# Tokens stationary in every projection, features reached by a trip through device memory, and VectorE for the gate product of the second MLP

## What is computed

```
h = h + stick_breaking_mixer(rms_norm(h, norm_mix), sb_w_qkv, sb_w_o)      # 16 heads of 128
h = h + square(relu(rms_norm(h, norm_mlp) @ mlp_w1)) @ mlp_w2             # 2048 -> 8192 -> 2048
x = rms_norm(h, final_norm)
z = rms_norm(x, pre_mix_g_2) @ w_in_2                                     # q, k, v: 1024 each, pool: 1024
m = concat(chunked_attention(q, k, v, rel_bias_2), multiscale_pool(u)) @ w_o_2
x = x + rms_norm(m, post_mix_g_2)
up = causal_dwconv(rms_norm(x, pre_ffn_g_2) @ w_up_2, conv_w_2, conv_b_2)  # 2048 -> 2 x 5632
y = (gelu(up[:5632]) * up[5632:]) @ w_down_2
out = x + rms_norm(y, post_ffn_g_2)
```

## Time and profile before

| | |
|---|---|
| median of 3 runs | 2119.08 us (2118.93 to 2119.95) |
| profiled execution, first to last instruction | 2117.7 us |
| TensorE busy | 2110.5 us (100%), 10990 matmuls |
| VectorE, ScalarE, GpSimd busy | 1259.2, 1049.5, 189.2 us |
| moved by DMA | 415.11 MB, mean 196 GB/s |

### The profile page before, as it was taken

One profiled execution on the slowest core, in us unless ns is written; L12 is line 12 of the kernel. 1 busy time (PEld: TensorE's weight loads), 2 busy tenths in 40 slices (PEclk: granted clock), 3 DMA queues, 4 the chain that ended last, 5 costly groups with the idle time before them and its releaser, 6 DMA issues.

```text
span 2117.7 us, 26776 instructions
## 1 busy us (share of the span) xinstructions
PE 2110.5 (100%) x10990; PEld 1810.4 (85%) x10990; DVE 1259.2 (59%) x1341; ACT 1049.5 (50%) x1222; POOL 189.2 (9%) x90
## 2 busy tenths in 40 slices
PE   9999999999999999999999999999999999999998
PEld 8888888888888888888888888888888888888887
DVE  6555656656455555465667755576666644566565
ACT  7554555544334443344555635465455443455543
POOL 3000000000000000000004000002222100222210
PEclk9999999999999999999999999999999999999999
DMA  8565557765666666666676567655655666556663
GB/s 289 171 207 172 180 169 232 223 195 174 209 193 183 199 211 191 186 193 195 219 238 189 178 210 228 195 183 173 195 191 178 217 191 192 182 175 199 204 210 120
DMA packets 220363, 415.11 MB, mean 196 GB/s; under 512 B 13521, under 2 KB 23889, under 8 KB 219729
## 3 DMA queue, kind: packets, MB, share of 16 engines
q1 hardware_dynamic: 219376, 408.92, 61.3%
q10 hardware_dynamic: 864, 4.49, 0.6%
HBM read 405.49 MB, written 7.86 MB: 195 GB/s over the span
## 4 chain that ended last, share of the span: by engine, by line
PE 100%; ACT 0%; DVE 0%; issue 0%; POOL 0%; DVEq 0%; POOLq 0%
PE ps L1503 99%; PE ps L1506 0%; ACT T L1075 0%; DVE QK L1390 0%; ACT raw L1088 0%; ACT aHL L954 0%; ACT zs L1085 0%; DVE rs L1407 0%; POOL ones L1434 0%; ACT rs L1080 0%; POOL ident L1432 0%; DVE rs L1404 0%; DVE rs L1409 0%; DVE rs L1399 0%; POOL tri L1433 0%
## 5 line engine op out<-in xcount | busy, mean ns | idle before, releaser
L1146 DVE TENSOR_TENSOR Wl<-raw,Wh 128x1024 fp32r<-128x1024 f32 x743 | 911.8, 1246 | 640.6 <-ACT Wh L930 639.9
L1503 PE MATMUL ps<-aHL,Wh 128*128 128x512 f32 x3336 | 1158.7, 392 | 0.5 <-ACT aHL L954 0.4
L930 ACT ACTIVATE Wh<-raw 128x1024 fp32r<-128x1024 f32 x743 | 767.6, 1054 | 588.9 <-PE ps L1503 585.4
L1503 PE MATMUL ps<-aHL,Wl 128*128 128x256 f32 x3328 | 929.3, 279 | 0.0
L1503 PEld LDWEIGHTS ps<-aHL,Wh 128*128 128x128 f32 x3336 | 624.2, 187 | 139.5 <-issue 0.9
L1503 PEld LDWEIGHTS ps<-aHL,Wl 128*128 128x128 f32 x3328 | 628.2, 189 | 0.5
L1503 PE MATMUL ps<-Wh,hid 128*128 128x512 f32 x1728 | 533.1, 389 | 0.0
L1503 PEld LDWEIGHTS ps<-Wh,hid 128*128 128x128 f32 x1728 | 324.4, 188 | 67.5
L1503 PE MATMUL ps<-Wl,hid 128*128 128x512 f32 x864 | 336.2, 389 | 0.0
L1503 PEld LDWEIGHTS ps<-Wl,hid 128*128 128x128 f32 x864 | 162.2, 188 | 33.5
L1503 PE MATMUL ps<-Wh,oHL 128*128 128x512 f32 x512 | 158.7, 389 | 0.0
(11 more groups left out here) (175 smaller groups left out, 792.2 us busy)
## 6 DMA issues: line engine op xcount, KB each, us to landing
raw<-in_mlp_w_dram SPq DMA_DIRECT2D x256, 512.0 KB, 4.3
raw<-in_w_up_dram SPq DMA_DIRECT2D x176, 512.0 KB, 3.9
raw<-in_sb_w_qkv_dram SPq DMA_DIRECT2D x93, 512.0 KB, 4.8
raw<-in_w_down_dram SPq DMA_DIRECT2D x88, 512.0 KB, 4.2
raw<-in_w_in_dram SPq DMA_DIRECT2D x64, 512.0 KB, 4.4
raw<-in_sb_w_o_dram SPq DMA_DIRECT2D x32, 512.0 KB, 5.3
raw<-in_w_o_dram SPq DMA_DIRECT2D x32, 512.0 KB, 4.3
passed_rows<-xN SPq DMA_DIRECT2D x16, 256.0 KB, 4.3
```

The costliest lines, as they stand in the source:

```text
L930: e.activation(Wh[:, i % NW, :], rawv[:, i % NRAW, :], ACT.Copy).then_inc(st["hi"][0], 1)
L1146: e.tensor_tensor(Wl[:, i % NW, :], rawv[:, i % NRAW, :], Wh[:, i % NW, :].bitcast(F32), ALU.subtract).then_inc(st["lo"][0], 1)
L1503: return e.matmul(o, l, r, start=start, stop=stop, skip_group_check=True)
```

## The change

All strips are of kind N. The column groups of the weights that feed q, k, the pool and both up projections are permuted on the host, and their results leave PSUM by a trip: ScalarE copies the token rows, scaled by a column of norm factors (or relu, then square), to T0; SP writes them to device memory (`passed_strip`, two slots); two pieces later SP reads them back in blocks into T0; two pieces after that VectorE transposes T0 into QK, T1 or E. One trip may be on its way at a time; a second one is put off until the first has landed. Rows r_a and r_b, `diagonal`, `spread` and the "wide" products go. Columns scaled by QSCALE are made beside the norm factors.

PSUM is cut anew: two sets of two banks for strips, one of four banks for side work and the pool's own piece. Scores, weights and values move back by three pieces (five for the first group). The output projections and w_down run the first two strips as a pair: both strips' pieces but the last two, then those two of each. `mixed_norm` and the turns after w_o_2 use the side set. In the second MLP VectorE makes the gate product, the steps of the convolution move closer together, and the halves follow one piece later, as before.

The diff, cut to its core:

```diff
     def side_set():
-        return 1 - now[0]
+        return 2
+    def strip_pair(w, s4, ks, tail, mov, tiles, evacs, koff=0):
+        first, n = len(p.pieces), len(ks) - tail
+        for i in range(2):
+            strip(w, (s4 + i) * STRIP, ks, mov, tiles, evacs[i], koff)
+        a, b = p.pieces[first:first + len(ks)], p.pieces[first + len(ks):]
+        p.pieces[first:] = a[:n] + b[:n] + a[n:] + b[n:]
+        return first
...
+    def trip(s, k, n, how, col, need, landed_to):
+        if st.get("landing"):
+            st["landing"].append(lambda: trip(s, k, n, how, col, need, landed_to))
+            return
+        st["landing"] = [lambda: landed_to(moved)]
...
+        step("stage_rows", n=n, set=s, mm=k, how=how, col=col, need=need, t0_free=list(free["T0"]), staged=staged, squared=squared,
+             passed=passed, held=st.get(("trip", n % 2)))
+        st["trip", n % 2] = moved
+        free[f"set{s}"] = [staged[1]]
+        free["T0"] = [moved]
+        def back():
+            step("land_rows", n=n, passed=passed, done=moved)
+            later(2, landed)
...
+        later(2, back)
...
-    after(13, r_job("r1", "a", "r_a"))
+    after(13, lambda: rms("r1", "a"))
...
-        after(first["v", g] + 1, sb_scores(g))
-        after(first["v", g] + 8, sb_weights(g))
-        after(first["v", g] + 12, values(g, 1))
+        at = first["v", g] + (0 if g else 2)
+        after(at + 4, sb_scores(g))
+        after(at + 11, sb_weights(g))
+        after(at + 15, values(g, 1))
...
-        after(first2["v", g] + 1, sm_scores(g))
-        after(first2["v", g] + 10, sm_turn(g))
-        after(first2["v", g] + 12, values(g, 2))
+        after(first2["v", g] + 4, sm_scores(g))
+        after(first2["v", g] + 13, sm_turn(g))
+        after(first2["v", g] + 15, values(g, 2))
...
-        ps = [ctx.enter_context(nc.psum_tensor(f"ps{i}", [128, 4, 512], F32)) for i in range(2)]
+        ps = [ctx.enter_context(nc.psum_tensor(f"ps{i}", [128, n, 512], F32)) for i, n in enumerate((2, 2, 4))]
...
+                elif k == "stage_rows":
+                    if st["held"]:
+                        e.wait_ge(*st["held"])
+                    for t in range(2):
+                        e.wait_ge(*(st["squared"] or st["staged"])[t])
+                        e.dma_start(passed_strip[st["n"] % 2, t * 128:(t + 1) * 128, :], strip_rows[:, t, :]).then_inc(st["passed"][0], 16)
+                elif k == "land_rows":
+                    e.wait_ge(*st["passed"])
+                    for a in range(4):
+                        e.dma_start(strip_landed[a * 32:(a + 1) * 32, :, :],
+                                    passed_strip[st["n"] % 2].rearrange("(c j) (a f) -> a j c f", c=8, a=4)[a]).then_inc(st["done"][0], 16)
...
+                elif k == "turn_strip":
+                    for t in st["need"]:
+                        e.wait_ge(*t)
...
+                    e.transpose(dst, strip_blocks).then_inc(st["done"][0], 1)
...
-                elif k == "gate":
-                    e.tensor_tensor(E4, E4, Z4, ALU.mult).then_inc(st["done"][0], 1)
+                elif k == "gate":
+                    e.tensor_tensor(E4, E4, Z4, ALU.mult).then_inc(st["done"][0], 1)
...
-                    for m in range(4):
-                        c = slice(t * 512 + m * 128, t * 512 + (m + 1) * 128)
-                        mm(P[:, m, :], wh[:, c], x, q["first"] and t == 0, False)
-                        r = mm(P[:, m, 0:TOK], wl[:, c], x[:, 0:TOK], False, q["last"] and t == 1)
+                    for row in range(2):
+                        hi = mov[:, kt + t, row * 128:(row + 1) * 128]
+                        lo = mov[:, kt + t, TOK + row * 128:TOK + (row + 1) * 128]
+                        mm(P[:, row, :], hi, wh[:, c], q["first"] and t == 0, False)
+                        mm(P[:, row, :], hi, wl[:, c], False, False)
+                        m = mm(P[:, row, :], lo, wh[:, c], False, False)
```

More of the change, by code:

```diff
@@ L140, in row_pair @@
         second = dict(root=done("rms_root"), rec=done("rms_rec"), sq=done("rms_rec"), prod=done("rms_rec"), r=done("rms_r"))
[L141 to L145, removed]
+        both, scaled = done("rms_r"), done("rms_r")
+        step("row_pair", need=st["rows_sq"], total=total, mean=mean, first=first,
+             square=square, moved=moved, mean2=mean2, second=second, both=both, scaled=scaled)
+        st["r3c"], st["r4c"] = first["r"], scaled
     def turn(n, gain_name, need):
@@ L169, in turn_blocks @@
             tile_hl[4 * n:4 * n + 4] = lo
+            waiting, st["moving"] = st["moving"][1:], []
+            for job in waiting:
+                job()
         later(3 if n == 3 else 4, turn_blocks)
[L172 to L183, removed]
+    def trip(s, k, n, how, col, need, landed_to):
+        if st.get("landing"):
+            st["landing"].append(lambda: trip(s, k, n, how, col, need, landed_to))
+            return
+        st["landing"] = [lambda: landed_to(moved)]
+        staged = [done("rows_staged") for t in range(2)]
+        squared = [done("rows_squared_up") for t in range(2)] if how == "relu" else None
+        passed, moved = done("strip_passed", 32), done("strip_moved", 4 * 16)
+        step("stage_rows", n=n, set=s, mm=k, how=how, col=col, need=need, t0_free=list(free["T0"]), staged=staged, squared=squared,
[6 more added lines that the diff above has]
+            later(2, landed)
+        def landed():
+            first, *others = st["landing"]
+            st["landing"] = []
+            first()
+            for job in others:
+                job()
+        later(2, back)
@@ L191, in common, with evac_qk, landed, go @@
         return summed, kw
-    def evac_qk(which, g, scale, r, rname):
+    def evac_qk(which, g, col, rname):
+        n = next_trip()
         def f(s, k):
[L195 to L203, removed]
+            def landed(moved):
+                turned = done("qk_turned")
+                step("turn_strip", to="qk", g=g, which=which, need=[moved, *free[f"qk{g % 2}"], *(free["QK1"] if g == 1 else [])],
+                     done=turned)
+                free["T0"] = [turned]
+                st["k" if which else "q", g] = turned
+            def go():
+                trip(s, k, n, "copy", col, [st[rname]], landed)
@@ L354, in evac_pool, with landed @@
     def evac_pool(u):
+        n = next_trip()
         def f(s, k):
[L356 to L360, removed]
+            def landed(moved):
+                turned = done("win_turned")
+                step("turn_strip", to="E", need=[moved, *free["E"]], done=turned)
+                free["T0"] = [turned]
                 rounds = []
@@ L561, in gated, with go @@
                 later(1, halves)
-            later(0 if "r6" in st else 4, scaled)
+            def go():
+                trip(s, k, n, "copy", "b", [st["r6"]], landed)
+            if "r6" in st:
+                go()
+            else:
+                later(2, go)
         return f
@@ L683, in plan_program @@
         need = []
-        if q["first"]:
+        if q["kind"] == "P":
+            need += free["set2"]
+        elif q["first"]:
             now[0] = 1 - now[0]
+            set_of[q["strip"]] = now[0]
             need += free[f"set{now[0]}"]
@@ L693, in plan_program @@
                 need.append(tok)
-        q["set"], q["n"] = now[0], i
+        q["set"], q["n"] = 2 if q["kind"] == "P" else set_of[q["strip"]], i
         if i < N - HELD:
             step("products", i=i, need=need, lo=(lo_sem, i + 1), rows=(0, 1), row0=q["kind"] == "N" and q["last"],
-                 half=half[i][2] if i < 3 else None, row=st["r1"] if q["wide"] else None)
+                 half=half[i][2] if i < 3 else None)
             k = (mm_sem, i + 1)
```

285 lines of the change are left out of this document (133 added, 152 removed).

## The result

The changed kernel takes 2251.61 us (median; 2245.16 to 2253.42), the kernel before 2119.09 us: 6.2% longer, ratio 1.062 with a 95% interval of 1.0603 to 1.0633. The prediction was 2096.0, range 2091 to 2107.

A forecast was written before the change was run, and what follows sets the result against it. TensorE, busy 2110.5 of 2117.7 us, was taken as the bound. Span: 2117.7 - 22.0 - 3.1 + 2.0 = 2094.6 us; with 1.4 us from span to median, 2096.0, range 2091 to 2107.

The forecast's parts named there:

- Item 1: Projections: 415 pieces go from weights stationary (T) to tokens stationary (N), 2.773 to 2.720 us each, saving 22.0 us.
- the 2 us for the scores: First attention, group 0: TensorE waits for late trips ahead of the scores, 2 us added, range 0 to 4.
- D: Rival: projections with aHL stationary run 2 ns a matmul slower; gain 12.0 in place of 22.0 us, 2106; chance 0.05.
- Item 2: TensorE's path: four dummy r_a products and three spread products vanish, 0.44 us each, saving 3.1 us.
- C: Rival: the cut into 16 matmuls is not why T pieces are slow; only 4 + 3.1 us go, 2114; chance 0.05.
- Item 4: The 52 strips' trips: 11.7 us each for the whole move, waits on VectorE and SP covered, costing nothing.
- Rival B: SP's trip waits hold back weight loads, the raw buffers run dry; 2146 at 1 us a strip; chance 0.07.
- item 5: DMA queues: trips raise the mean share from 0.61 to at most 0.88; nothing lost, but little room.
- Item 7: Consumers moved later: no cost except at scores, with 1.8 us to spare in four groups and a 2 us wait in the first.
- rival A: Late scores in more groups if trips run 2 to 3 us longer: 8 to 12 us, 2102 to 2107; chance 0.14.
- Item 3: Other engines' work, gate product on VectorE (13.5 us) included: covered by TensorE's 2094 us, costed at nothing.
- item 6: PSUM cut into smaller strip sets plus a side set: removes waits, but TensorE has none to remove; worth nothing.

The follow-up runs named there:

- e7: Changed kernel with e1's pad, transposes and scores placed later, and the second MLP's older taps moved behind three weight splits: 2094.53 us, ratio 0.9883 to the kernel before.
- e1: Changed kernel with an unused tensor of 1920 bytes a partition ahead of rs, restoring the SBUF addresses of the kernel before: 2221.6 us.
- e12: e7 without its pad, so with the changed kernel's SBUF addresses: 2149.97 us, ratio 1.014 to the kernel before.

## Why the prediction was wrong

**Item 1 (kind T to kind N): right, at the old addresses.** In e7, where no wait is left that the kernel before did not have, but for 0.3 us at a group of scores and 0.6 at a split, the span is 2092.7 us. The prediction's sum without the 2 us for the scores is 2117.7 - 22.0 - 3.1 = 2092.6. The intervals of aHL and hid pieces are alike there (226.8 and 226.6 ns in the mean of all undisturbed ones), so D is refuted. Item 2 (3.1 us) stands with it; the two were only measured together. C is refuted: with only 7 us saved e7 would have been at 2112, or 2114 with the wait of 2 us.

**What item 1 lacked: the place of the tiles.** The step reads "the source of the stationary tokens hardly matters", from rows that all lay on multiples of 256 bytes. The diff drops two tiles ahead of them, and I costed that at nothing without saying so. It is 51 us of the miss of 149 (2243.4 against 2094.6 of span); the waits and what follows them are 97. No row of the kernel before could price it, but the diff's allocations showed that aHL, hid and oHL move by 1920 bytes, and this should have been named as an unknown.

**Item 4 (the trip's length): wrong, the main failure.** "The way out is issued by about +1.1" and "so they cost nothing" were worked out for a strip with empty queues. The row of the whole move was too short everywhere: in the first MLP a trip took 12.1 to 14.9 us from the way out's issue to the transpose, not 10.5. VectorE stood 2.5 to 5.4 us for each, and the cover held, so the 16 relu strips cost no gap. (With the faster strips of e1 they cost 0.8 us.) In w_up three things differ. The staging stands behind the gelu and two splits, and came 8 us after the strip's end where the prediction had it done by +0.7; in 10 of the 12 strips of the first part it came 8 to 10 us after. SP's way out stands behind a load that waits for a split. After the transpose come 2.08 us of newest taps ahead of the Wh splits and 3.23 us of older taps between Wl splits, and the prediction had only splits there. The ways back landed in a median of 4.1 us, not 2.6. From the way out's issue to the transpose lie 11 to 14 us (13.45 in the turn shown; 16.9 once), not 10.5. So the transpose of the turn shown started 23.6 us after the strip's end, not 10.5. Each lateness delays the next staging; it isn't paid once but goes round, and TensorE waits in nearly every strip.

**The clock.** A gap was priced at its own length. The 64 us of gaps in the second MLP brought 24 us more, 13 of them in starts 427 ns apart at the lower clock. The Trainium skill ("TensorE: Matmul & The Clock Gate", section "HAM oscillation — how this bites in real kernels") describes such a cold penalty when waits recur in a loop; the trace agrees, with starts 427 ns apart behind a wait of 3.03 us, and its rule for the lower level (same page, section "Wait — 56ns, not 53.3ns?": columns / 1.2 GHz) gives the same 427 ns.

**Rival B: the right sign and nearly the right place.** It named SP's waits and the raw ring, and gave 2146 at 1 us a strip. Apart from the scores the gaps came only in the 22 strips of w_up, at about 4 us each with the clock, and through VectorE's and ScalarE's queues rather than SP's alone. At 0.07 its chance was too small: what I held against it ("loads land in 3.9 us", no gap at a share of 0.97) says that the DMA engines have room, and nothing on the order in the queues. The DMA share agrees with item 5: 0.717 in e7 against 0.613, and it did no harm.

**Item 7 and rival A.** The gap at the first scores was 4.4 us of waiting, not 2, and three other groups waited too (two of the first mixer, one of the second), 8.8 us in all. The 1.8 us to spare was too little for trips that take 12 to 17 us from way out to transpose among the first mixer's own work.

**Item 3, items 5 and 6.** They hold as far as they speak of busy time: no engine became the bound (VectorE 59% in e7). But item 3's "if no single hand-over is late" did not hold, and the gate product on VectorE was a gain of 31 us inside the ring, where I had it at nothing. Nothing here tests item 6 by itself; no wait for a PSUM set shows in e7.

## What to carry to other kernels

When a diff drops or adds a tile, look at where the tiles that TensorE reads come to lie; here multiples of 256 bytes were the fast places, and a pad brought them back. When a result comes back after a round trip, here of some 12 us, follow every in-order queue that its consumer passes through, for two successive strips: if the late consumer stands ahead of work that its own producer needs, the lateness goes round. Put the work that feeds TensorE ahead of the late consumer, even where the engines have 40% to spare.

## What the hardware showed that was not expected

- The interval of back-to-back fp32r matmuls depends on the address of the activations in SBUF: 226.7 ns (512 columns) on a multiple of 256 bytes, 232.4 at 128 over (233.1 in e12, at the same place), 233.3 at 64 over (15 triples in 10.50 us), whether they are stationary or streaming (pairs of 512 and 256 columns: 346.6 ns against 351.1). Why, and whether Wh and Wl count likewise, was not tried.
- A wait of 2 to 3 us can bring TensorE to 1.2 GHz for the next few us: starts lie 427 ns apart for about 5 us behind the 3.03 us gap that ends at 1585.70. In the second MLP all five waits for Wl from 3.0 us up were followed by 6 to 12 such starts, and four of the nine between 2.0 and 2.8 us; the other five by none.
